# A two-block transformer step on one core: weights split in chunks of 128x1024, the low part written over the loaded chunk

## What is computed

```
mod = silu(c) @ ada_w + ada_b                     # 2048 x 12288, a single row times a matrix
sh1, sc1, g1, sh2, sc2, g2 = split(mod, 6)
u = rms_norm(h, norm_mix_g) * (1 + sc1) + sh1
h = h + g1 * (hybrid_mixer(u @ w_in, ...) @ w_out)
u = rms_norm(h, norm_ffn_g) * (1 + sc2) + sh2
h = h + g2 * ((silu(u @ w_gate) * (u @ w_up)) @ w_down)      # inner width 5632
x = rms_norm(h, final_norm_g)
for i in (0, 1):                                  # the second block, two layers
    if i == 1: k, v = split(h @ w_kv_shared)
    u = h @ w_in_2[i]; mk, mv = split(mem @ w_mem_kv[i])
    mixed = concat(branch(u) * silu(gate_b), memory_attention(u, mk, mv) * silu(gate_m))
    h = layer_norm(alpha * h + mixed @ w_out_2[i])
```

## Time and profile before

| what | value |
|---|---|
| three timed executions | 2325.42, 2327.52, 2329.5 us (median 2327.52) |
| span of the profiled execution | 2324.9 us |
| PE busy | 2105.9 us (91%), 9820 matmuls |
| DVE busy | 1503.5 us (65%), 2632 instructions |
| ACT busy | 1063.4 us (46%), 1931 instructions |
| POOL busy | 117.8 us (5%) |
| bytes moved | 486.09 MB, 209 GB/s on average |

### The profile page before, as it was taken

The page is one execution under the profiler, slowest core; times in us unless marked ns, Lnnn a source line. Parts: engine busy times, 40 slices in busy tenths (PEclk is TensorE's granted clock), DMA queues, the critical chain, the costliest instruction groups (busy, mean ns, idle before and its releaser), DMA issues.

```text
span 2324.9 us, 29571 instructions
## 1 busy us (share of the span) xinstructions
PE 2105.9 (91%) x9820; PEld 1731.4 (74%) x9820; DVE 1503.5 (65%) x2632; ACT 1063.4 (46%) x1931; POOL 117.8 (5%) x188
## 2 busy tenths in 40 slices
PE   6928999998798999999999999799799699999797
PEld 4817888776576887888888888588578578888675
DVE  5988888656898877555555556755345755555466
ACT  3414444466334544445544554455334445555542
POOL 2000000221003000000000000100000300000000
PEclk9958999999899999999999999899899899999998
DMA  9986998523796997666656665466526356664462
GB/s 299 387 297 230 359 320 312 172 80 89 278 335 203 293 292 244 199 191 190 189 188 194 190 189 186 132 196 193 166 78 226 109 168 194 190 197 138 154 218 99
DMA packets 321589, 486.09 MB, mean 209 GB/s; under 512 B 33696, under 2 KB 145536, under 8 KB 320064
## 3 DMA queue, kind: packets, MB, share of 16 engines
q1 hardware_dynamic: 318704, 468.63, 62.6%
q0 software_dynamic: 2768, 15.98, 1.9%
HBM read 465.13 MB, written 2.10 MB: 201 GB/s over the span
## 4 chain that ended last, share of the span: by engine, by line
PE 75%; DVE 11%; issue 6%; SPq 3%; DMA 2%; ACT 2%; POOL 0%; DVEq 0%; POOLq 0%; ACTq 0%
PE ps L444 23%; PE ps L446 23%; PE ps L445 23%; DVE ada_acc L385 4%; SPq L812 3%; DVE w_lo L370 3%; PE ps L483 1%; PE ps L696 1%; PE ps L659 1%; ACT w_hi L338 1%; DMA raw<-in_w_mem_kv 1%; PE ps L1311 1%; PE ps L643 1%; DVE evac L551 1%; DMA raw<-in_w_out 1%
## 5 line engine op out<-in xcount | busy, mean ns | idle before, releaser
L370 DVE TENSOR_TENSOR w_lo<-raw,w_hi 128x512 fp32r<-128x512 f32 (+1 forms) x1328 | 919.1, 703 | 628.4 <-ACT w_hi L338 626.2
L338 ACT ACTIVATE w_hi<-raw 128x512 fp32r<-128x512 f32 (+1 forms) x1328 | 829.4, 629 | 1004.4 <-PE ps L446 893.0
L444 PE MATMUL ps<-w_hi,actT 128*128 128x512 f32 (+1 forms) x2304 | 915.1, 397 | 60.3 <-DVE actT L558 24.4
L446 PE MATMUL ps<-w_hi,actT 128*128 128x512 f32 (+1 forms) x2304 | 901.7, 391 | 0.0
L445 PE MATMUL ps<-w_lo,actT 128*128 128x512 f32 (+1 forms) x2304 | 901.2, 391 | 0.0
L444 PEld LDWEIGHTS ps<-w_hi,actT 128*128 128x128 f32 x2304 | 437.4, 190 | 162.2 <-DVE actT L558 27.9
L446 PEld LDWEIGHTS ps<-w_hi,actT 128*128 128x128 f32 x2304 | 437.0, 190 | 92.1
L445 PEld LDWEIGHTS ps<-w_lo,actT 128*128 128x128 f32 x2304 | 438.3, 190 | 88.5 <-issue 1.4
L385 DVE SCALAR_TENSOR_TENSOR ada_acc<-raw,c_col,ada_acc 128x512 f32<-128x512 f32 x360 | 271.7, 755 | 11.7 <-DMA raw<-in_ada_w 2.3
L444 PE MATMUL ps<-w_hi,hidT 128*128 128x512 f32 x352 | 137.7, 391 | 2.8 <-DVE w_lo L370 2.8
L446 PE MATMUL ps<-w_hi,hidT 128*128 128x512 f32 x352 | 137.0, 389 | 0.0
(11 more groups left out here) (212 smaller groups left out, 1056.6 us busy)
## 6 DMA issues: line engine op xcount, KB each, us to landing
raw<-in_w_in SPq DMA_DIRECT2D x216, 512.0 KB, 4.1
raw<-in_ada_w SPq DMA_DIRECT2D x192, 512.0 KB, 5.6
raw<-in_w_out SPq DMA_DIRECT2D x96, 512.0 KB, 4.9
raw<-in_ffn_w_gate SPq DMA_DIRECT2D x176, 256.0 KB, 2.9
raw<-in_ffn_w_up SPq DMA_DIRECT2D x176, 256.0 KB, 3.1
raw<-in_ffn_w_down SPq DMA_DIRECT2D x88, 512.0 KB, 4.1
raw<-in_w_kv_shared SPq DMA_DIRECT2D x48, 512.0 KB, 3.7
raw<-in_w_mem_kv SPq DMA_DIRECT2D x32, 512.0 KB, 8.8
```

What stands on the lines that cost most here:

```text
L338: act.activation(w_hi[:, g, 0:w], raw[:, slot, b, 0:w], ACT.Copy).then_inc(hi_ready, 1)
L370: nc.vector.tensor_tensor(w_lo[:, g, 0:w], raw[:, slot, b, 0:w], w_hi[:, g, 0:w].bitcast(f32), ALU.subtract).then_inc(blocks_read, 1)
L444: nc.tensor.matmul(o, hi, w_hi[:, g, 0:w], start=(k == 0), stop=False)
L446: last = nc.tensor.matmul(o, lo, w_hi[:, g, 0:w], start=False, stop=(k == nk - 1))
```

## The change

Everything that is split is now a whole chunk. `w_hi` has four chunks (8 blocks) instead of four blocks, ACT rounds 128x1024 in one instruction and DVE subtracts 128x1024 in one. The low part has no buffer of its own any more: it is written over the chunk in `raw`, and `w_hi` takes the bytes that both had. PE waits once for each chunk and gives back a chunk at a time. So a slot with weights is free only when PE is through with it; a slot with `ada_w` is free after DVE's two steps, as before. Hooks and leads of both blocks of a chunk are now called ahead of the chunk.

```diff
-RING, HILO = 8, 4
+RING, HI = 8, 4
...
-        r_hilo = region(2 * HILO * NC * 4)
-        w_hi = at("w_hi", [P, HILO, NC], f32r, r_hilo)
-        w_lo = at("w_lo", [P, HILO, NC], f32r, r_hilo + HILO * NC * 4)
+        w_lo = at("w_lo", [P, RING, 2, NC], f32r, 0)
+        r_hilo = region(HI * 2 * NC * 4)
+        w_hi = at("w_hi", [P, HI, 2, NC], f32r, r_hilo)
...
+        def slot_free(sp, st, p, first, j, off):
+            per = st.per[0]
+            n = st.start[0] + st.local[j][0] + off - RING + (0 if first else per)
+            if n < 0:
+                return
+            if loaded[n] == "w":
+                done, each = HI + loaded[:n + 1].count("w"), st.per[1]
+                sp.wait_ge(parts_used, done if first else done - each + p * each)
+            else:
+                done, each = 2 * loaded[:n + 1].count("a"), 2 * (per - st.per[1])
+                sp.wait_ge(ada_step, done if first else done - each + p * each)
...
-                        sp.wait_ge(blocks_read, pl.kb + off + 2)
+                        slot_free(sp, st, p, first, j, off)
...
-                        for b in range(2):
-                            k = 2 * ch + b
+                        for k in (2 * ch, 2 * ch + 1):
                             if hooks and k in hooks and not (first and j == 0):
...
-                            act.wait_ge(parts_used, pl.gb + k + 1)
-                            g = (st.local[j][1] + k) % HILO
-                            act.activation(w_hi[:, g, 0:w], raw[:, slot, b, 0:w], ACT.Copy).then_inc(hi_ready, 1)
+                        act.wait_ge(parts_used, pl.gb + ch + 1)
+                        g = (st.local[j][1] + ch) % HI
+                        act.activation(w_hi[:, g, :, 0:w], raw[:, slot, :, 0:w], ACT.Copy).then_inc(hi_ready, 1)
...
-                                nc.vector.tensor_tensor(w_lo[:, g, 0:w], raw[:, slot, b, 0:w],
-                                                        w_hi[:, g, 0:w].bitcast(f32),
-                                                        ALU.subtract).then_inc(blocks_read, 1)
+                            nc.vector.tensor_tensor(w_lo[:, slot, :, 0:w], raw[:, slot, :, 0:w],
+                                                    w_hi[:, g, :, 0:w].bitcast(f32),
+                                                    ALU.subtract).then_inc(lo_ready, 1)
...
-                            pe.wait_ge(blocks_read, 2 * RING + pl.kb + off + b + 1)
-                            g = (st.local[j][1] + k) % HILO
+                            if b == 0:
+                                pe.wait_ge(lo_ready, pl.gb + ch + 1)
+                            g = (st.local[j][1] + ch) % HI
...
-                            last.then_inc(parts_used, 1)
+                        last.then_inc(parts_used, 1)
```

More of the change, by code:

```diff
@@ L98 @@
         _s.local.append((k, g, n, a))
-        k += _nk * len(_kind)
-        g += _nk * ("w" in _kind)
+        k += _nk // 2 * len(_kind)
+        g += _nk // 2 * ("w" in _kind)
         n += "w" in _kind
@@ L249, in program @@
         w_loaded = [S(f"w_loaded{i}") for i in range(RING)]
-        blocks_read = S("blocks_read")
+        ada_step = S("ada_step")
         hi_ready = S("hi_ready")
+        lo_ready = S("lo_ready")
         parts_used = S("parts_used")
@@ L264, in chunks, with slot_of @@
                     yield k, ch, off
-                    off += 2
+                    off += 1
+        def slot_of(st, j, off):
+            return (st.start[0] + st.local[j][0] + off) % RING
+        loaded = "".join(k for st in STAGES for _ in range(st.bodies)
+                         for kd, nk in st.panels for k in kd * (nk // 2))
+        def slot_free(sp, st, p, first, j, off):
[9 more added lines that the diff above has]
+                sp.wait_ge(ada_step, done if first else done - each + p * each)
         def stage_loads(sp, name, w_src, a_src=None, width=NC):
@@ L271, in body @@
                 for j in range(len(st.panels)):
-                    pl = place(st, p, j)
                     for kind, ch, off in chunks(st, j):
-                        slot = ((st.start[0] + st.local[j][0] + off) // 2) % RING
-                        sp.wait_ge(blocks_read, pl.kb + off + 2)
+                        slot = slot_of(st, j, off)
+                        slot_free(sp, st, p, first, j, off)
                         if kind == "w":
@@ L293, in program @@
                 for kind, ch, off in chunks(st, j):
-                    s = ((st.start[0] + st.local[j][0] + off) // 2) % RING
+                    s = slot_of(st, j, off)
                     cnt[s] += 32 if st.name.startswith("gu") and kind == "w" else 16
@@ L331, in body @@
                                 lead[k]()
-                            if b == 0:
-                                wait_chunk(act, st, p, j, idx)
-                            slot = ((st.start[0] + st.local[j][0] + off) // 2) % RING
-                            act.wait_ge(parts_used, pl.gb + k + 1)
-                            g = (st.local[j][1] + k) % HILO
-                            act.activation(w_hi[:, g, 0:w], raw[:, slot, b, 0:w], ACT.Copy).then_inc(hi_ready, 1)
+                        wait_chunk(act, st, p, j, idx)
+                        slot = slot_of(st, j, off)
+                        act.wait_ge(parts_used, pl.gb + ch + 1)
+                        g = (st.local[j][1] + ch) % HI
+                        act.activation(w_hi[:, g, :, 0:w], raw[:, slot, :, 0:w], ACT.Copy).then_inc(hi_ready, 1)
             run_bodies(act, st, body)
@@ new lines, in body @@
+                        wait_chunk(dve, st, p, j, idx)
+                        for k in (2 * ch, 2 * ch + 1):
+                            if k == 0:
+                                nc.vector.tensor_scalar(acc, raw[:, slot, 0, :], c_col[:, 0:1], None,
+                                                        ALU.mult).then_inc(ada_step, 1)
+                            else:
+                                dve.wait_ge(ada_step, pl.an * KD + k)
+                                nc.vector.scalar_tensor_tensor(acc, raw[:, slot, k % 2, :], c_col[:, k:k + 1], acc,
+                                                               ALU.mult, ALU.add).then_inc(ada_step, 1)
@@ L443, in body @@
                                 o = ps[:, bank + t, 0:w]
-                                nc.tensor.matmul(o, hi, w_hi[:, g, 0:w], start=(k == 0), stop=False)
-                                nc.tensor.matmul(o, hi, w_lo[:, g, 0:w], start=False, stop=False)
-                                last = nc.tensor.matmul(o, lo, w_hi[:, g, 0:w], start=False, stop=(k == nk - 1))
-                            last.then_inc(parts_used, 1)
+                                nc.tensor.matmul(o, hi, w_hi[:, g, b, 0:w], start=(k == 0), stop=False)
+                                nc.tensor.matmul(o, hi, w_lo[:, slot, b, 0:w], start=False, stop=False)
+                                last = nc.tensor.matmul(o, lo, w_hi[:, g, b, 0:w], start=False, stop=(k == nk - 1))
+                        last.then_inc(parts_used, 1)
             run_bodies(pe, st, body)
@@ L454, in panel_done @@
             pl = place(st, p, j)
-            eng.wait_ge(parts_used, HILO + pl.gb + st.panels[j][1])
+            eng.wait_ge(parts_used, HI + pl.gb + st.panels[j][1] // 2)
         def bank_of(st, j):
@@ L1176, in _ @@
         def _(pe):
[L1177 removed]
+            pe.sem_inc(parts_used, HI)
             pe.wait_ge(S("ident"), 1)
```

22 lines of the change are left out of this document (5 added, 17 removed).

## The result

The changed kernel takes 2335.41 us, median of seven runs (2328.97 to 2339.82), against 2326.63 us for the kernel before, also seven runs (2321.83 to 2329.5): ratio 1.0042, interval 1.0027 to 1.0057. A second set of five runs gave 2332.77 us and a ratio of 1.0037 (1.0024 to 1.0051). So it is slower by 0.4%. The forecast was 2325.2 us; the measured time lies inside the range of 2311 to 2341, on the side that had a chance of 0.25. A small gain was forecast and a loss clear of noise was measured: the step that failed is the unit in which PE waits (Step 1 of the prediction), together with a term of Step 5 that was half its size or less.

A forecast was written before the change was run, and what follows sets the result against it. PE was taken to bound the kernel (75% of the chain), with DVE the bound in wout. The terms summed to -2.3 us on the profiled span of 2324.9; with 2.6 us added, 2325.2 us, range 2311 to 2341.

The forecast's parts named there:

- Step 1: Splits: half as many, longer instructions, a mixed pair costing DVE about 0.07 us less; -1.5 us in wout (0 to -3).
- the side that had a chance of 0.25: Whole kernel: slower by more than 0.2%, chance 0.22 + 0.03.
- Step 5: Load ring: weight slots held until PE is through; +2 us in mixed panels and +2.4 us at the start.
- Step 1's bracket in the sum: POOL's second load of x, in wout: falls where PE is dry behind DVE anyway, so counted as nothing.
- Step 2: PE starts later after running dry: +2.5 us at five places (0.5 to 3.5), +1.0 us in three down stages.
- Step 3: Eight blocks ahead instead of four: down2 -1.5 us, win and gu0 -1.8, shorter splits ahead of five stages' first low -0.6.
- Step 4: DVE against GpSimd: fewer DVE instructions held by POOL operations; -3.5 us in kv (-8.5 to +1.5), -1.3 in in0.
- Step 5, first part: Mixed panels: loads issued later, landing time L taken as 5.4 to 5.8 us; +2 us over 13 panels (0 to +15).
- the rival of 2342 us: Mixed stages become bound by landing, L staying at 6.6 us; +18 us over memkv, win and win_end; chance 0.22.
- that of 2314.5 us: kv and in0 stalls shrink by one POOL operation less each, loads land fast, no wait in the ring; -13 us; chance 0.20.
- Step 5, second part: Start of memkv: chunk 4 loaded later, less reserve beside POOL's 2 MB load of x; PE late by +2.4 us (+1 to +5).

The follow-up runs named there:

- blocks: The changed kernel with rounding, subtraction and PE's waits back to 128x512 blocks; long slot lifetime and eight rounded blocks kept; 2318.75 us, 0.9974 to the kernel before.
- pe_whole: As blocks, but PE waits once for both subtracted blocks of a chunk; ACT and DVE still 512 wide; 2330.18 us, 1.0016 to the kernel before.
- shallow: As blocks, but with four rounded blocks instead of eight; 2329.96 us, 1.0019 to the kernel before.
- late_x: The changed kernel with POOL's 2 MB load of x issued only when PE has done chunk 26 of 32 of memkv; 2334.9 us, 1.0047 to the kernel before.
- pieces: As blocks, with POOL's loads cut up: x in eight 256 KB pieces in memkv, x and bias in quarters in wout; 2315.01 us, 0.9943 to the kernel before.
- before_pieces: The kernel before the change, with POOL's loads cut up as in pieces; 2322.7 us, 0.9993 to the kernel before.

## Why the prediction was wrong, point by point

The sum was -2.3 us; the medians say +8.8 and +7.1 in the two sets. (The 2.6 us that the sum then adds for what lies around the span are 1.7 in every execution that has both numbers; that moves the forecast by 0.9 us and not its sign.) By its own steps:

- **Step 1, -1.5 us for `wout`: the sign was wrong.** `wout` lost 3.3 to 3.5 us. As DVE's occupation my 1.14 us held: four subtractions in a row take 4.63 us, the last of them 1.22, so they start 1.14 us apart, and nine of the 512-wide ones take 5.50, 0.60 apart. But a single one lasts 1.22 to 1.24 us until PE may use it. The Trainium skill ("VectorE: DVE Perf Modes", section on the TRN2 errata) has (N + 151) / 0.96 ns for a `tensor_tensor` in fp32, an estimate of 1.22 us for 1024; this case's trace agrees, 1.23 us in the first panel of `kv`. So the way from the rounding to PE did not get shorter, and for PE, which waits for the whole chunk, it got longer. The timelines of DVE in `down2`, of the changed kernel and then of `blocks`:

```profile
1417.36 4.63 DVE L384 TENSOR_TENSOR w_lo<-raw,w_hi 128x1024 fp32r<-128x1024 f32 x4 [0.26 <-ACT w_hi L353]
```

```profile
1407.76 5.50 DVE L385 TENSOR_TENSOR w_lo<-raw,w_hi 128x512 fp32r<-128x512 f32 x9
```

  And the premise, that DVE bounds all of `wout`, was a misreading of an average. PE's waits for DVE from 640 to 712 us in the kernel before are three:

```profile
PE ps L444 <- DVE w_lo L370: 7.3, 3, 3.3
```

  Away from them PE's steps are the same in both kernels: the third and the fourth panel begin with 2.72, 2.72, 2.72, 3.18, 3.16 us. So there was nothing for 32 pairs to save. PE stands still behind one burst of DVE in each of three panels and behind a load, and that stall is then ended by a whole chunk. I had it "paid at the end once". The three gaps behind bursts were 3.71, 2.53 and 2.18 us and are 3.11, 3.31 and 3.64, and the twelve matmuls behind them took 4.45, 4.19 and 2.86 us and take 4.13, 4.33 and 4.45: about half of the 3 us lost there is the lower clock. By panels `wout` is at -2.4, +2.1, +0.8 and +3.0 us; the gain in the first one is in `blocks` too. `pe_whole`, with PE's wait alone, has 2.5 us more than `blocks`.
- **Step 1's bracket in the sum, POOL's second load of x at nothing, was wrong too.** The chain of the changed kernel in `wout`:

```profile
620.42 11.37 DMA raw<-in_w_out
...
631.81 1.06 ACT w_hi L353
...
632.90 1.24 DVE w_lo L384
```

  The kernel before had two gaps there, of 1.42 and 2.95 us; the changed one has one of 5.50 us.
- **Step 2, +2.5 and +1.0 us: right in kind.** The starts of three stages came 0.53 us later each, `down0`, `down1` and the first panel of `down2` lost 0.45 each: 2.9 us where I can point at them. What I missed is that a whole chunk is also what ends a stall in `wout` and in the stages where groups are split between the blocks, and that the lower clock can come with it. `pe_whole` puts the price of the whole chunk as PE's unit at 11.4 us, where my Steps 1 and 2 had 2.
- **Step 3: right on the lookahead.** `down2` won 1.8 us, 0.74 in each of three panels less what Step 2 counts (-1.5 forecast), and its waits for `w_lo` fell from 1.3 us to the one row below. `win` and `gu0` together won 0.2 to 0.4 us (-1.8, range to +1.5). Of the 0.6 us for shorter splits ahead of the first `low` some 0.3 is there, before `win` and `gu0`; before `kv` it is 0.14 us the other way. Not foreseen: `win_end` and `out1` won 4 and 1.5 us. By `shallow` against `blocks` the lookahead is worth 11 us, the largest gain of the change.

```profile
PE ps L458 <- DVE w_lo L384: 0.2, 1, 0.2
```

- **Step 4, -3.5 and -1.3 us: too large for `kv`.** `kv` won 0.6 us and `in0` 0.9 (or lost 1.1, in `late_x`). The timeline of DVE in the first panel of `kv`, of the changed kernel:

```profile
1848.36 5.31 DVE L384 TENSOR_TENSOR w_lo<-raw,w_hi 128x1024 fp32r<-128x1024 f32 x1 [1.05 <-ACT w_hi L353]
1853.60 0.98 DVE L565 TENSOR_SCALAR evac<-ps,cols 128x256 f32<-128x256 f32 x2
1854.50 4.08 DVE L572 TENSOR_TENSOR actT<-evac,actT 128x512 fp32r<-128x512 f32 x1
1858.51 5.58 DVE L384 TENSOR_TENSOR w_lo<-raw,w_hi 128x1024 fp32r<-128x1024 f32 x1
1864.02 0.98 DVE L565 TENSOR_SCALAR evac<-ps,cols 128x256 f32<-128x256 f32 x2
1864.93 4.70 DVE L572 TENSOR_TENSOR actT<-evac,actT 128x512 fp32r<-128x512 f32 x2
```

  The rule was right: each POOL operation lets one instruction of two tensors by, and one of 1024 costs no more than one of 512, 5.31 and 5.58 us. But POOL's four operations now take 20.5 us (1848.02 to 1868.48) instead of 19.4, and four of DVE's instructions are held as before: a chunk, a `low`, a chunk, a `low`. PE's waits in `kv`, of the kernel before (1840 to 1875 us) and then of the changed one (1840 to 1880):

```profile
PE ps L444 <- DVE actT L558: 14.8, 2, 12.4
```

```profile
PE ps L458 <- DVE actT L572: 13.4, 2, 8.0
```

  So the first wait did get shorter by one POOL operation, 4.4 us, as forecast. But the second gap grew from 2.87 to 5.82 us. The last held `low` ends 0.9 us later than I had it, with POOL's longer run, and the chunk behind it, which I had at 2.72 us, took 4.76, at the lower clock. These two, 0.9 and 2.0 us, are the gain that is missing; a slow chunk stood there before, too (4.32 us), and my sum had none. In `in0` the gap of 8.23 us became two of 3.73 and 2.04. That the width helps is not shown: `blocks`, 512 wide, won 1.0 us in `kv`.
- **Step 5, first part, +2 us: the other way.** I took L at 5.4 to 5.8 us; it fell to a median of 4.3 in `win`, which fits fewer loads in flight, and `win` and `win_end` got shorter. (My 13 mixed panels are 12.) So the rival of 2342 us, on whose side the result lies, had the wrong mechanism; that of 2314.5 us needed one more POOL operation less in `kv` and `in0` each, and all gaps together fell by 1.4 and 2.5 us only.
- **Step 5, second part, +2.4 us: the term that was mis-sized.** It was 5.4 and 7.7 us. Two things were left out. The load in flight takes 10.5 us, not the 8.7 to 9.4 of the earlier trace rows (beside x it took 9.8 before, too), so that PE has a gap of 5.2 us; and behind it a chunk runs at the lower clock, 2.2 us more. It is also not a matter of the ring's start (`late_x`), but of each slot's lifetime beside a load of 2 MB (`shallow`, `pieces`, `before_pieces`).

By the medians the change comes apart in four: the slot's lifetime +4.4 us (`shallow`), eight blocks of lookahead -11.2 (`blocks`), PE's wait for whole chunks +11.4 (`pe_whole`), the 1024-wide instructions, with side work ahead of the chunk, on top 2.6 to 5.2 (the two sets of the changed kernel). Each difference of two kernels is uncertain by 3 to 4 us, worked out from the intervals of their ratios, so the last one can hardly be told from zero. Only the difference between whole steps is shown by these runs; how the last term falls to ACT and DVE, and to width and side work, is not parted.

## What to carry to other kernels

Count the unit in which the bound engine waits apart from the width of the instructions that feed it: joining two blocks costs little in work, but a stall then ends one block later, and here that was some 11 us of 2326, as much as all the lookahead bought with the memory saved. When a buffer is freed later, look for the largest transfer that shares its queues' bandwidth and compare its length with the reserve; here it helped to cut that transfer up and not to shift it. And price a gap on PE with the chunk behind it, not by its length alone.

## What the runs showed of the hardware that I had not expected

- A 1024-wide subtraction takes 1.22 to 1.24 us by itself, but in a row they start 1.14 us apart; 512-wide ones take 0.69 us and start 0.60 apart. So two small ones in a row cost 0.06 us more than a wide one and hand over the first half 0.5 us earlier.
- Two gaps of the same length on PE, 2.18 us each behind the last burst of `wout`, had different ends: from the start of the first to that of the twelfth matmul behind it were 2.63 us in the kernel before and 4.18 us in `blocks`. The windows of the two (columns as in rows 2), before and then `blocks`:

```profile
706.70:709.30 2.60, 2.60 (x13) 2.10 (x12) 2.56 (x5) 0.63 (x1) 0.00 (x0) 1.00 0.49 134
```

```profile
701.90:706.10 4.20, 4.20 (x12) 3.29 (x13) 4.13 (x7) 2.30 (x4) 0.00 (x0) 0.59 0.89 292
```

  The granted clock is 0.59 on average in the second, 1.00 in the first. That such gaps also spread the times of executions is likely and not shown.
- One load of 2 MB beside the ring goes with landings of 9.8 us in the kernel before, 10.1 in `blocks` and 10.4 in the changed one; eight of 256 KB, spaced out, with 6.9 us in `pieces`. Behind it they are, in the changed kernel from 60 to 90 us, the same stage:

```profile
DMA to landing us min/median/max: 3.9/4.4/4.7
```

  That is half the 8.8 us of the earlier trace rows, in a stage that moves 360 GB/s instead of 387.
